# Where the output norm of the first linear-attention mixer is made: tile by tile inside its loop, or behind it

## The chip, the cores and the metric

The kernel runs on one core of one Trainium2 chip, in one launch. The metric is the device time of a run in microseconds (us); of the kernel before there are three runs, and their median counts. Beside them stands one profiled execution, from which all durations below are taken. PE is TensorE, PEld its weight loads, DVE VectorE, ACT ScalarE, POOL GpSimd and SP SyncE, which here issues most of the DMAs.

## The reference

The model has two layers on 512 tokens of width 1024. Layer 0 mixes the tokens with two linear attentions side by side, layer 1 with a sliding-window attention, and a mixture of 16 experts stands behind either. The change is in the first of the two linear attentions (gla below), whose chunks hold 64 tokens, with 4 heads of 64 key and 128 value columns:

```python
def gla_chunked(q, k, v, g):
    b = jnp.cumsum(g, axis=-2)
    b_last = b[..., -1:, :]
    q_dec = q * jnp.exp(b)
    k_dec = k * jnp.exp(-b)
    a = jnp.where(incl, jnp.einsum('bhnid,bhnjd->bhnij', q_dec, k_dec), 0.0)
    o_intra = jnp.einsum('bhnij,bhnjv->bhniv', a, v)
    upd = jnp.einsum('bhncd,bhncv->bhndv', k * jnp.exp(b_last - b), v)
    ...                        # state = dec * state + upd, chunk by chunk
    return o_intra + jnp.einsum('bhncd,bhndv->bhncv', q_dec, s_prev)

    ...
    oa = rms_norm(oa, gla_norm) * jax.nn.silu(za...)     # per token and head, over 128 values
    ...
    return o @ w_out
```

`rms_norm(x, gain)` is `x * rsqrt(mean(x*x) + 1e-6) * gain`. The norm of `oa` and its product with the gate are what the change moves.

## The kernel before

The kernel goes through stages one behind another. Between two stages PE, ACT and DVE each drain and wait for one another (the semaphore `phase_done`). The gla stage is the second of them, between the projection of layer 0 and the second linear attention (gdn). The order of the instructions on each engine is that in which the code is written, one program for each engine, with semaphores between them; `Steps` objects count them, and `X.at(t, name)` is the value at which step `name` of tile t is done.

The gla stage works on four tiles t of 128 tokens, each of two chunks c of 64. PSUM has eight banks of 128x512 words. In the loop over t:

- PE turns queries and keys of the next tile into bank 6 (`gla_turn`, L934, waits for `kz` of the tile before), multiplies the masked scores with the values into bank t (L1093, waits for `A`), adds the part of the state for chunk 0 (L1103, `int0`), makes the scores of the next tile in bank 7 (`gla_scores`, L1069), adds the part of the state for chunk 1 (L1103, `int1`, waits for `s0`), and makes the state's updates of the next tile in banks 4 and 5 (`gla_updates`, L1078). The second of these waits for `s1` of this tile, since DVE still reads bank 5 until then.
- DVE masks the scores (`A`, L2233), scales the next tile's queries and keys (`gla_qk`, L2212 and L2216), brings the state over chunk 0 (`s0`, L2241, four instructions, waits for `int0`), makes the next tile's scaled key rows (`gla_k_rows`, L2223, two instructions), and brings the state over chunk 1 (`s1`, L2241, waits for `int1`).
- ACT squares the four heads of bank t with their sums (`gla_sq`, `sm_g[:, 0]`, waits for `int1`). It does nothing else in the loop. All ACT instructions stand on L1566, a helper.

Behind the loop DVE first does one step of another job, the sums of a modulation vector (`mix_sides(1)`, L2055; its inputs come by SP, the load for the step three further on waits for this one). Then comes the norm of all four tiles at once: DVE `var` (L2250, 128x16), ACT the inverse root, DVE a Newton step of four instructions (`newton`, L2032, L2034, L2036, L2038, each waiting for the one before), then DVE 16 products of output, root and gate into `on_g` (L2257, 128x128 each, out of bank t), PE four transposes for each tile into bank 4+t (L934, waiting for `on` of the tile), and ACT a copy of each into `oT` (128x512). `on_g` holds the gate `silu(za)` times the gain beforehand. In the names of the profile `on_g` is in ring, `sm_g` and the state in work, `oT` in hT.

Of the kernel before, what the change touches and what calls it, by code (L numbers as in the profile page):

```python
# [15 lines left out]
P = 128  # L16
# [4 lines left out]
EPS = 1e-6  # L21
# [94 lines left out]
def build_block(nc, a, out):  # L116
    ctx = ExitStack()
    with ctx:
# [147 lines left out]
        GLA_PE = Steps(sem("gla_pe"), ["o", "int0", "int1"])  # L266
        GLA_DVE = Steps(sem("gla_dve"), ["A", "s0", "s1"])
        GLN_PE = Steps(sem("gla_norm_pe"), ["oT"])
        GLN_ACT = Steps(sem("gla_norm_act"), ["ss0", "ss1", "ss2", "ss3", "root", "oT0", "oT1", "oT2", "oT3"])
        GLN_DVE = Steps(sem("gla_norm_dve"), ["var", "n1", "n2", "n3", "rstd", "on0", "on1", "on2", "on3"])  # L270
        PRE_DVE = Steps(sem("gdn_pre_dve"), ["u", "au", "mx", "g", "lnb", "lk", "lq", "lbk", "pre", "colj"])
        PRE_ACT = Steps(sem("gdn_pre_act"), ["e", "l", "expa", "lnss", "exp"])
        PRE_PE = Steps(sem("gdn_pre_pe"), ["cum"])
# [656 lines left out]
        def _(pe):  # L930
# [141 lines left out]
            def gla_updates(t):  # L1072
                pe.wait_ge(GLP_DVE.sem, GLP_DVE.at(t, "ku"))
                for c in range(2):
# [4 lines left out]
                                 start=True, stop=True)  # L1079
                    ins.then_inc(GLP_PE.sem, GLP_PE.one(f"u{c}"))  # L1080

            def gla():

                gla_gates()
# [3 lines left out]
                for t in range(TT):  # L1088
# [16 lines left out]
                        ins.then_inc(GLA_PE.sem, GLA_PE.one(f"int{c}"))  # L1105
                    if t + 1 < TT:
                        gla_updates(t + 1)
                for t in range(TT):
                    pe.wait_ge(GLN_DVE.sem, GLN_DVE.at(0, f"on{t}"))
                    for hd in range(HEADS):  # L1110
                        ins = turn(bank(4 + t)[:, cols(hd)], on_g[:, t, hd])
                    ins.then_inc(GLN_PE.sem, GLN_PE.one("oT"))

            def gdn_pre():
                pe.wait_ge(PRE_DVE.sem, PRE_DVE.at(0, "g"))
# [448 lines left out]
        def _(act):  # L1564
# [140 lines left out]
            def gla():  # L1705
                act.wait_ge(const_in, 16)
                act.wait_ge(GATE_PE.sem, GATE_PE.at(0, "z"))
                f(gate_a, ps[:, 2:4].rearrange("p a b -> p (a b)"), ACT.Abs).then_inc(GATE_ACT.sem, GATE_ACT.one("abs"))
                act.wait_ge(GATE_ACT.sem, GATE_ACT.at(0, "abs"))
                f(gate_e, gate_a, ACT.Exp, scale=-1.0).then_inc(GATE_ACT.sem, GATE_ACT.one("e"))  # L1710
                act.wait_ge(GATE_ACT.sem, GATE_ACT.at(0, "e"))
                f(gate_e, gate_e, ACT.Ln, bias=1.0).then_inc(GATE_ACT.sem, GATE_ACT.one("l"))
                act.wait_ge(GATE_PE.sem, GATE_PE.at(0, "cums"))
                f(eb_all, ps[:, 4:8, 0:256], ACT.Exp, scale=1.0 / 16).then_inc(GATE_ACT.sem, GATE_ACT.one("eb"))
                f(enb_all, ps[:, 4:8, 0:256], ACT.Exp, scale=-1.0 / 16).then_inc(GATE_ACT.sem, GATE_ACT.one("enb"))
                f(ekb_all, ps[:, 4:8, 256:512], ACT.Exp, scale=1.0 / 16).then_inc(GATE_ACT.sem, GATE_ACT.one("ekb"))
                table(ACT.Abs_reciprocal_sqrt)
                for t in range(TT):
                    act.wait_ge(GLA_PE.sem, GLA_PE.at(t, "int1"))
                    for hd in range(HEADS):  # L1720
                        ins = f(gla_sq[:, t, cols(hd)], bank(t)[:, cols(hd)], ACT.Square,
                                accum_out=sm_g[:, 0, HEADS * t + hd:HEADS * t + hd + 1])
                    ins.then_inc(GLN_ACT.sem, GLN_ACT.one(f"ss{t}"))
                act.wait_ge(GLN_DVE.sem, GLN_DVE.at(0, "var"))
                f(sm_g[:, 2], sm_g[:, 1], ACT.Abs_reciprocal_sqrt).then_inc(GLN_ACT.sem, GLN_ACT.one("root"))
                for t in range(TT):
                    act.wait_ge(GLN_PE.sem, GLN_PE.at(t, "oT"))
                    f(oT[:, 0:HEADS, cols(t)], bank(4 + t, HEADS, P)).then_inc(GLN_ACT.sem, GLN_ACT.one(f"oT{t}"))

            def gdn_pre():  # L1730
                act.wait_ge(PRE_DVE.sem, PRE_DVE.at(0, "au"))
# [295 lines left out]
        def _(dve):  # L2027
# [191 lines left out]
            def gla_k_rows(t):  # L2219
# [3 lines left out]
                    ins = v.tensor_tensor(ku[r, t % 2, c], pqk[r, t, 256:512], ekb_all[r, t], ALU.mult)  # L2223
                ins.then_inc(GLP_DVE.sem, GLP_DVE.one("ku"))

            def gla():
                gla_gates()
                gla_qk(0)
# [2 lines left out]
                for t in range(TT):  # L2231
                    dve.wait_ge(GLP_PE.sem, GLP_PE.at(t, "A"))
                    v.copy_predicated(at_g, mask, bank(7, HEADS, P)).then_inc(GLA_DVE.sem, GLA_DVE.one("A"))  # L2233
                    if t + 1 < TT:
                        gla_qk(t + 1)
                    for c in range(2):
# [7 lines left out]
                        ins.then_inc(GLA_DVE.sem, GLA_DVE.one(f"s{c}"))  # L2244
                        if c == 0 and t + 1 < TT:
                            gla_k_rows(t + 1)
                        dve.wait_ge(GLA_DVE.sem, GLA_DVE.at(t, f"s{c}"))
                mix_sides(1)
                dve.wait_ge(GLN_ACT.sem, GLN_ACT.at(0, "ss3"))
                v.tensor_scalar(sm_g[:, 1], sm_g[:, 0], 1.0 / DV, EPS, ALU.mult, ALU.add).then_inc(GLN_DVE.sem, GLN_DVE.one("var"))  # L2250
                dve.wait_ge(GLN_ACT.sem, GLN_ACT.at(0, "root"))
                dve.wait_ge(GLN_DVE.sem, GLN_DVE.at(0, "var"))
                newton(GLN_DVE, 0, sm_g[:, 2], sm_g[:, 1], sm_g[:, 3])
                for t in range(TT):
                    for hd in range(HEADS):
                        n = HEADS * t + hd
                        ins = v.scalar_tensor_tensor(out=on_g[:, t, hd], in0=bank(t)[:, cols(hd)], scalar=sm_g[:, 2, n:n + 1],  # L2257
                                                     in1=on_g[:, t, hd], op0=ALU.mult, op1=ALU.mult)
                    ins.then_inc(GLN_DVE.sem, GLN_DVE.one(f"on{t}"))

            def gdn_pre():
                D_ = PRE_DVE
# [652 lines left out]
```

## Time and profile before

| | us |
|---|---|
| runs of the kernel, median of 3 | 1502.57 |
| lowest and highest of them | 1500.47, 1505.88 |
| the profiled execution, its own time | 1498.98 |
| its span in the trace | 1496.8 |
| the loop over t and the norm behind it, to the last copy | about 298 to 334 |

The span is the time from the first to the last instruction in the trace; 2.2 us of the profiled execution lie around it. A row of the timeline is a run of like instructions: its start, the time from the first's start to the last's end, engine, line, operation, the tiles out<-in, the count, and in brackets the idle time of the engine before it with what ended that.

### The profile page before, as it was taken

How to read it: one execution, taken by the hardware profiler on the slowest of the kernel's cores; microseconds unless marked ns; L12 is line 12 of the kernel's file. 1: busy time of each engine (PE TensorE's matmuls, PEld its weight loads, DVE VectorE, ACT ScalarE, POOL GpSimd, SP SyncE). 2: the span in 40 equal slices, each digit the busy share in tenths (PEclk: the TensorE clock that was granted, in tenths of full speed). 3: DMA queues.
4: the chain of work that ended last, by engine and by line, in shares of the span. 5: the costliest groups of instructions: out<-in, count | busy, mean ns of one | idle time of the engine just before them, and what ended most of it. 6: DMA issues, size and time to landing. Idle time of an engine off the chain costs nothing. (4 is left out here: it accounts for less than half of the span.)

```text
span 1496.8 us, 15648 instructions
## 1 busy us (share of the span) xinstructions
PE 1297.0 (87%) x6072; PEld 988.4 (66%) x6072; DVE 1090.4 (73%) x1325; ACT 699.3 (47%) x894; POOL 335.6 (22%) x130
## 2 busy tenths in 40 slices
PE   4799889566989986999999977986898699999992
PEld 1488777346986455888888864443445588888882
DVE  3757766575876464898899966777346499999994
ACT  2212332324135132777777743225613277777770
POOL 2100000000000001466666520000000145445541
PEclk9779999797999977999999997997997799999996
DMA  9678433701030254899999927346006489999954
GB/s 339 236 258 288 157 99 120 259 23 63 15 127 31 111 217 178 326 392 386 382 382 378 350 80 299 113 159 233 1 28 236 143 333 380 376 377 391 383 201 183
DMA packets 63888, 338.17 MB, mean 226 GB/s; under 512 B 11866, under 2 KB 12394, under 8 KB 49732
## 3 DMA queue, kind: packets, MB, share of 16 engines
q1 hardware_dynamic: 51428, 311.00, 55.7%
q0 software_dynamic: 11568, 22.91, 4.4%
q10 hardware_dynamic: 816, 3.23, 0.6%
q8 instruction: 50, 0.82, 0.2%
q14 instruction: 26, 0.21, 0.0%
HBM read 325.63 MB, written 28.84 MB: 237 GB/s over the span
## 5 line engine op out<-in xcount | busy, mean ns | idle before, releaser
L1410 PE MATMUL ps<-ring_r,work_r 128*128 128x512 f32 x536 | 211.5, 395 | 0.0
L830 POOL TENSOR_TENSOR work<-work,early_mod 128x1024 f32<-128x1024 f32 x30 | 169.7, 5656 | 145.5 <-ACT work L1566 145.5
L2434 DVE TENSOR_TENSOR ring_r<-ring,early_mod_r 128x2048 fp32r<-128x2048 f32 x76 | 182.4, 2433 | 27.1 <-ACT early_mod_r L1566 26.6
L1408 PE MATMUL ps<-early_mod_r,work_r 128*128 128x512 f32 x468 | 187.9, 401 | 7.7 <-DVE work_r L2737 4.7
L1409 PE MATMUL ps<-early_mod_r,work_r 128*128 128x512 f32 x468 | 183.6, 392 | 0.0
L1566 ACT ACTIVATE work<-ps 128x512 f32<-128x512 f32 (+4 forms) x123 | 80.2, 663 | 214.2 <-PE ps L1410 133.4
L1566 ACT ACTIVATE work_r<-ring 128x2048 fp32r<-128x2048 f32 (+2 forms) x87 | 133.5, 1557 | 55.4 <-PE ps L943 55.4
L934 PE MATMUL ps<-const,work 128*128 128x128 f32 x712 | 106.4, 292 | 49.6 <-DVE work L2550 12.2
L1566 ACT ACTIVATE early_mod_r<-ring 128x2048 fp32r<-128x2048 f32 x79 | 147.6, 1911 | 0.3 <-PE ps L1410 0.2
L934 PEld LDWEIGHTS ps<-const,work 128*128 128x128 f32 x712 | 90.1, 150 | 74.1 <-issue 14.7
L1408 PE MATMUL ps<-work_r 128*128 128x512 f32 x324 | 131.5, 406 | 6.8 <-DVE work_r L2737 4.7
L2434 DVE TENSOR_TENSOR ring_r<-ring,work_r 128x2048 fp32r<-128x2048 f32 x52 | 124.1, 2413 | 5.6 <-ACT work_r L1566 5.6
L1409 PE MATMUL ps<-work_r 128*128 128x512 f32 x324 | 128.1, 395 | 0.0
L1410 PEld LDWEIGHTS ps<-ring_r,work_r 128*128 128x128 f32 x536 | 102.0, 190 | 22.5
L1278 PE MATMUL ps<-ring,hT 128*128 128x512 f32 x256 | 111.1, 593 | 1.4 <-ACTq L2018 0.7
L1408 PEld LDWEIGHTS ps<-early_mod_r,work_r 128*128 128x128 f32 x468 | 88.3, 189 | 28.4 <-DVE work_r L2737 7.1
L822 POOL DMA_INDIRECT work<-h_rows,row_i x32 | 66.8, 2087 | 165.6 <-PE ps L934 118.1
L1409 PEld LDWEIGHTS ps<-early_mod_r,work_r 128*128 128x128 f32 x468 | 88.6, 189 | 17.1
L1278 PEld LDWEIGHTS ps<-ring,hT 128*128 128x128 f32 x256 | 48.2, 190 | 60.9 <-issue 58.4
L1302 PE MATMUL ps<-ring,hT 128*128 128x512 f32 x192 | 86.1, 608 | 1.9 <-ACT hT L1566 1.9
L1566 ACT ACTIVATE work_r<-ps 128x512 fp32r<-128x512 f32 (+1 forms) x66 | 53.5, 812 | 66.2 <-PE ps L934 66.2
L835 POOL DMA_DIRECT2D h_rows<-work x8 | 4.3, 541 | 348.2 <-DVE work L2424 348.2
(331 smaller groups left out, 2575.4 us busy)
## 6 DMA issues: line engine op xcount, KB each, us to landing
ring<-in_moe_w_up_dram SPq DMA_DIRECT2D x33, 2048.0 KB, 9.9
early_mod<-in_ada_w_dram SPq DMA_DIRECT2D x80, 512.0 KB, 4.6
ring<-in_moe_w_gate_dram SPq DMA_DIRECT2D x19, 2048.0 KB, 9.3
hT<-in_moe_w_down_dram SPq DMA_DIRECT2D x16, 2048.0 KB, 9.0
ring<-in_moe_w_down_dram SPq DMA_DIRECT2D x15, 2048.0 KB, 9.6
work<-in_moe_w_gate_dram SPq DMA_DIRECT2D x14, 2048.0 KB, 10.1
ring<-in_ab_w_in_dram SPq DMA_DIRECT2D x7, 2048.0 KB, 9.5
ring<-in_ada_w_dram SPq DMA_DIRECT2D x4, 2048.0 KB, 23.3
```

What stands on the lines that cost most here:

```text
L822: nc.gpsimd.indirect_dma_start(xg[buf], None, h_rows[l], bass.IndirectOffsetOnAxis(rows_, 0), bounds_check=SEQ - 1, oob_is_err=False).then ...
L830: return nc.gpsimd.tensor_tensor(yb[buf], yb[buf], mod[:, 5 * D:6 * D], ALU.mult)
L835: nc.gpsimd.dma_start(h_rows[l][P * t:P * t + P, :], h[:, t]).then_inc(h_out, 16)
L934: return nc.tensor.transpose(dst, src, ident[0:k, 0:k])
L1278: ins = mm(bank((2 * t + n) % 3), oT[:, k, cols(t)], slot(c0 + n)[:, k], start=(k == 0), stop=(k == 7))
L1302: ins = mm(bank(j % 4), hT[:, k, cols(t)], slot(c)[:, k], start=(k == 0), stop=(k == 7))
L1408: mm(out, a_lo, w_hi, start=first_, stop=False)
L1409: mm(out, a_hi, w_hi, start=False, stop=False)
L1410: return mm(out, a_hi, w_lo, start=False, stop=last_)
L1566: return nc.scalar.activation(out, in_, fn, **kw)
L2434: v.tensor_tensor(half_of(l, m, half, True), half_of(l, m, half), highs[(2 * m + half) % MHIGHS].bitcast(F32), ALU.subtract).then_inc(SV.s ...
```

## The change

The norm is made for each tile by itself, one tile behind the loop, in place of all four behind it.

- DVE: `output_variance(t - 1)` stands behind the mask of tile t, `output_norm(t - 1)` (the Newton step on 128x4, and four of the 16 products) behind the key rows and ahead of `s1` of tile t. Behind the loop and behind `mix_sides(1)` stand both for the last tile.
- ACT: behind the squares of tile t it waits for `var` of that tile, makes its root, and copies the transposed output of tile t-1. Behind the loop it copies that of the last tile.
- PE: the four transposes of tile t-1 stand behind the updates of tile t+1, and go into bank t-1 in place of bank 4+t-1. Those of the last tile stand behind the loop.

The root and the Newton step are now made four times on four columns and not once on 16: DVE has 12 more instructions of the Newton step and 3 more of the variance, ACT 3 more roots.

```diff
-        GLN_ACT = Steps(sem("gla_norm_act"), ["ss0", "ss1", "ss2", "ss3", "root", "oT0", "oT1", "oT2", "oT3"])
-        GLN_DVE = Steps(sem("gla_norm_dve"), ["var", "n1", "n2", "n3", "rstd", "on0", "on1", "on2", "on3"])
+        GLN_ACT = Steps(sem("gla_norm_act"), ["ss", "root"])
+        GLN_DVE = Steps(sem("gla_norm_dve"), ["var", "n1", "n2", "n3", "rstd", "on"])
...
+            def turn_output_a(t):
+                pe.wait_ge(GLN_DVE.sem, GLN_DVE.at(t, "on"))
+                for hd in range(HEADS):
+                    ins = turn(bank(t)[:, cols(hd)], on_g[:, t, hd])
+                ins.then_inc(GLN_PE.sem, GLN_PE.one("oT"))
...
                     if t + 1 < TT:
                         gla_updates(t + 1)
-                for t in range(TT):
-                    pe.wait_ge(GLN_DVE.sem, GLN_DVE.at(0, f"on{t}"))
-                    for hd in range(HEADS):
-                        ins = turn(bank(4 + t)[:, cols(hd)], on_g[:, t, hd])
-                    ins.then_inc(GLN_PE.sem, GLN_PE.one("oT"))
+                    if t:
+                        turn_output_a(t - 1)
+                turn_output_a(TT - 1)
...
+                def put_output(t):
+                    act.wait_ge(GLN_PE.sem, GLN_PE.at(t, "oT"))
+                    f(oT[:, 0:HEADS, cols(t)], bank(t, HEADS, P))
+
                 for t in range(TT):
                     act.wait_ge(GLA_PE.sem, GLA_PE.at(t, "int1"))
                     for hd in range(HEADS):
                         ins = f(gla_sq[:, t, cols(hd)], bank(t)[:, cols(hd)], ACT.Square,
                                 accum_out=sm_g[:, 0, HEADS * t + hd:HEADS * t + hd + 1])
-                    ins.then_inc(GLN_ACT.sem, GLN_ACT.one(f"ss{t}"))
-                act.wait_ge(GLN_DVE.sem, GLN_DVE.at(0, "var"))
-                f(sm_g[:, 2], sm_g[:, 1], ACT.Abs_reciprocal_sqrt).then_inc(GLN_ACT.sem, GLN_ACT.one("root"))
-                for t in range(TT):
-                    act.wait_ge(GLN_PE.sem, GLN_PE.at(t, "oT"))
-                    f(oT[:, 0:HEADS, cols(t)], bank(4 + t, HEADS, P)).then_inc(GLN_ACT.sem, GLN_ACT.one(f"oT{t}"))
+                    ins.then_inc(GLN_ACT.sem, GLN_ACT.one("ss"))
+                    act.wait_ge(GLN_DVE.sem, GLN_DVE.at(t, "var"))
+                    own = slice(HEADS * t, HEADS * t + HEADS)
+                    f(sm_g[:, 2, own], sm_g[:, 1, own], ACT.Abs_reciprocal_sqrt).then_inc(GLN_ACT.sem, GLN_ACT.one("root"))
+                    if t:
+                        put_output(t - 1)
+                put_output(TT - 1)
...
                     v.copy_predicated(at_g, mask, bank(7, HEADS, P)).then_inc(GLA_DVE.sem, GLA_DVE.one("A"))
+                    if t:
+                        output_variance(t - 1)
                     if t + 1 < TT:
                         gla_qk(t + 1)
...
                         if c == 0 and t + 1 < TT:
                             gla_k_rows(t + 1)
+                        if c == 0 and t:
+                            output_norm(t - 1)
                         dve.wait_ge(GLA_DVE.sem, GLA_DVE.at(t, f"s{c}"))
                 mix_sides(1)
...
+                output_variance(TT - 1)
+                output_norm(TT - 1)
```

The order of DVE's instructions in the middle turn t = 1, before: mask, next tile's queries and keys, `s0`, key rows, `s1`, and the mask of t = 2.

```order
L2233 COPY_PREDICATED work<-early_mod,ps 128x512 [waits gla_prep_pe,gla_dve]
L2212 SCALAR_TENSOR_TENSOR work<-ps,ring 128x256 [waits gla_prep_pe]
L2216 TENSOR_TENSOR early_mod<-ps,ring 64x256 x2
L2241 SCALAR_TENSOR_TENSOR work<-work,ring,ps 64x128 [waits gla_pe]
L2241 SCALAR_TENSOR_TENSOR work<-work,ring,ps 64x128 x3
L2223 TENSOR_TENSOR work<-work,ring 64x256 x2
L2241 SCALAR_TENSOR_TENSOR work<-work,ring,ps 64x128 [waits gla_pe,gla_dve]
L2241 SCALAR_TENSOR_TENSOR work<-work,ring,ps 64x128 x3
```

And in the changed kernel, from the mask of t = 1 to the first instruction of `s1` (L2258 is the mask, L2238 the variance, L2268 `s0` and `s1`, L2232 the key rows, L2041 to L2047 the Newton step, L2247 the products).

```order
L2258 COPY_PREDICATED work<-early_mod,ps 128x512 [waits gla_prep_pe,gla_dve]
L2238 TENSOR_SCALAR work<-work 128x4 [waits gla_norm_act]
L2221 SCALAR_TENSOR_TENSOR work<-ps,ring 128x256 [waits gla_prep_pe]
L2225 TENSOR_TENSOR early_mod<-ps,ring 64x256 x2
L2268 SCALAR_TENSOR_TENSOR work<-work,ring,ps 64x128 [waits gla_pe]
L2268 SCALAR_TENSOR_TENSOR work<-work,ring,ps 64x128 x3
L2232 TENSOR_TENSOR work<-work,ring 64x256 x2
L2041 TENSOR_TENSOR work<-work 128x4 [waits gla_norm_dve,gla_norm_act]
L2043 TENSOR_TENSOR work<-work 128x4 [waits gla_norm_dve]
L2045 TENSOR_SCALAR work<-work 128x4 [waits gla_norm_dve]
L2047 TENSOR_TENSOR work<-work 128x4 [waits gla_norm_dve]
L2247 SCALAR_TENSOR_TENSOR ring<-ps,work,ring 128x128 [waits gla_norm_dve]
```

Four Newton instructions and four products (the last three of them follow in a row of their own) have come between the key rows and `s1`.

PE's instructions at the end of the turn t = 1, before: the updates of tile 2 for chunk 1, the turn of tile 3's queries and keys, and the scores times values of tile 2.

```order
L1078 MATMUL ps<-work 128x256 [waits gla_dve]
L1078 MATMUL ps<-work 128x256
L934 MATMUL ps<-const,work 128x128 [waits gla_prep_dve]
L934 MATMUL ps<-const,work 128x128 x3
L1093 MATMUL ps<-work 128x128 [waits gla_dve]
```

And in the changed kernel (L1099 stands where L1093 did).

```order
L1078 MATMUL ps<-work 128x256 [waits gla_dve]
L1078 MATMUL ps<-work 128x256
L934 MATMUL ps<-const,ring 128x128 [waits gla_norm_dve]
L934 MATMUL ps<-const,ring 128x128 x3
L934 MATMUL ps<-const,work 128x128 [waits gla_prep_dve]
L934 MATMUL ps<-const,work 128x128 x3
L1099 MATMUL ps<-work 128x128 [waits gla_dve]
```

The four transposes of tile 0's output have come between the updates and the next tile's turn; the same four for tile 1 stand in the next turn ahead of the scores times values of tile 3, and those of tile 2 behind the last `int1`.

## Rows read from the trace of the kernel before

**Rows 1.** The page: the span, and one DMA group with its median us to landing
```profile
span 1496.8 us, 15648 instructions
...
early_mod<-in_ada_w_dram SPq DMA_DIRECT2D x80, 512.0 KB, 4.6
```
**Rows 2.** The timeline, all engines, the turn t = 1 of the loop
```profile
303.38 1.13 PE L1078 MATMUL ps<-work 128*128 128x256 f32 x4 [0.53 <-DVE work L2241]
...
304.34 0.60 PE L934 MATMUL ps<-const,work 128*128 128x128 f32 x4
...
304.78 1.06 PE L1093 MATMUL ps<-work 128*128 128x128 f32 x8
...
305.77 1.08 PE L1103 MATMUL ps<-work 128*64 128x256 f32 x4
...
306.77 1.16 PE L1069 MATMUL ps<-work,early_mod 128*128 128x128 f32 x8
306.88 1.43 DVE L2241 SCALAR_TENSOR_TENSOR work<-work,ring,ps 64x128 f32<-64x128 f32 x4 [0.71 <-PE ps L1103]
308.34 0.85 DVE L2223 TENSOR_TENSOR work<-work,ring 64x256 f32<-64x256 f32 x2
...
308.37 1.08 PE L1103 MATMUL ps<-work 128*64 128x256 f32 x4 [0.43 <-DVE work L2241]
...
309.55 1.43 DVE L2241 SCALAR_TENSOR_TENSOR work<-work,ring,ps 64x128 f32<-64x128 f32 x4 [0.36 <-PE ps L1103]
...
311.03 1.13 PE L1078 MATMUL ps<-work 128*128 128x256 f32 x4 [0.53 <-DVE work L2241]
```
**Rows 3.** The timeline again, the last turn and the norm behind the loop
```profile
321.76 1.43 DVE L2241 SCALAR_TENSOR_TENSOR work<-work,ring,ps 64x128 f32<-64x128 f32 x4 [2.35 <-PE ps L1103]
...
323.24 1.08 PE L1103 MATMUL ps<-work 128*64 128x256 f32 x4 [1.52 <-DVE work L2241]
...
324.43 1.43 DVE L2241 SCALAR_TENSOR_TENSOR work<-work,ring,ps 64x128 f32<-64x128 f32 x4 [1.24 <-PE ps L1103]
...
327.54 0.18 DVE L2032 TENSOR_TENSOR work<-work 128x16 f32<-128x16 f32 x1 [0.28 <-ACT work L1566]
...
328.38 4.23 DVE L2257 SCALAR_TENSOR_TENSOR ring<-ps,work,ring 128x128 f32<-128x128 f32 x16
329.56 3.98 PE L934 MATMUL ps<-const,ring 128*128 128x128 f32 x16 [5.25 <-DVE ring L2257]
...
330.71 0.60 ACT L1566 ACTIVATE hT<-ps 128x512 f32<-128x512 f32 x1 [3.20 <-PE ps L934]
...
333.58 0.60 ACT L1566 ACTIVATE hT<-ps 128x512 f32<-128x512 f32 x1 [0.21 <-PE ps L934]
```
**Rows 4.** Groups by line and form: busy us, mean ns of one
```profile
L2257 DVE SCALAR_TENSOR_TENSOR ring<-ps,work,ring 128x128 f32<-128x128 f32 x16 | 4.2, 345 | 0.0
...
L2038 DVE TENSOR_TENSOR work<-work 128x4 f32<-128x4 f32 x4 | 0.6, 162 | 0.1
```
**Rows 5.** The timeline: DMA issues on SP, and small instructions of the next stage
```profile
327.20 10.28 SPq L712 DMA_DIRECT2D early_mod<-in_ada_w_dram  x2
...
335.85 4.06 DVE L2055 SCALAR_TENSOR_TENSOR x<-early_mod,par,x 128x1024 f32<-128x1024 f32 x3
...
343.21 0.17 DVE L2286 TENSOR_TENSOR work<-ps,work 128x16 f32<-128x16 f32 x1
343.30 0.17 DVE L2287 TENSOR_TENSOR work<-ps,work 128x16 f32<-128x16 f32 x1
```
**Rows 6.** Stretches: us, busy us of PE, PEld, DVE, ACT, POOL, PEclk, DMA, GB/s
```profile
322.00:324.00 2.00, 0.76 (x4) 0.47 (x4) 1.14 (x4) 0.00 (x0) 0.00 (x0) 1.00 0.00 0
...
328.00:330.00 2.00, 0.44 (x2) 0.44 (x3) 1.93 (x9) 0.00 (x0) 0.00 (x0) 0.50 0.72 207
...
350.00:355.00 5.00, 5.00 (x46) 5.00 (x45) 1.31 (x5) 1.02 (x2) 0.00 (x0) 0.98 0.00 0
```
**Rows 7.** The timeline: the scores of tile 0, ahead of the loop, at the lower clock
```profile
292.43 2.07 PE L1069 MATMUL ps<-work,early_mod 128*128 128x128 f32 x8 [1.28 <-DVE early_mod L2216]
```

More of the change, by code:

```diff
@@ L2224, in gla_k_rows, with output_variance, output_norm @@
                 ins.then_inc(GLP_DVE.sem, GLP_DVE.one("ku"))
+            def output_variance(t):
+                own = slice(HEADS * t, HEADS * t + HEADS)
+                dve.wait_ge(GLN_ACT.sem, GLN_ACT.at(t, "ss"))
+                v.tensor_scalar(sm_g[:, 1, own], sm_g[:, 0, own], 1.0 / DV, EPS, ALU.mult, ALU.add).then_inc(GLN_DVE.sem, GLN_DVE.one("var"))
+            def output_norm(t):
+                own = slice(HEADS * t, HEADS * t + HEADS)
+                dve.wait_ge(GLN_ACT.sem, GLN_ACT.at(t, "root"))
+                dve.wait_ge(GLN_DVE.sem, GLN_DVE.at(t, "var"))
+                newton(GLN_DVE, t, sm_g[:, 2, own], sm_g[:, 1, own], sm_g[:, 3, own])
+                for hd in range(HEADS):
+                    n = HEADS * t + hd
+                    ins = v.scalar_tensor_tensor(out=on_g[:, t, hd], in0=bank(t)[:, cols(hd)], scalar=sm_g[:, 2, n:n + 1],
+                                                 in1=on_g[:, t, hd], op0=ALU.mult, op1=ALU.mult)
+                ins.then_inc(GLN_DVE.sem, GLN_DVE.one("on"))
             def gla():
@@ L2246, in gla @@
                             gla_k_rows(t + 1)
+                        if c == 0 and t:
+                            output_norm(t - 1)
                         dve.wait_ge(GLA_DVE.sem, GLA_DVE.at(t, f"s{c}"))
                 mix_sides(1)
[L2249 to L2259, printed above, removed]
+                output_variance(TT - 1)
+                output_norm(TT - 1)
             def gdn_pre():
```

## The prediction

> **What bounds the kernel now.** The page's shares of busy time are means over a span of 1496.8 us [rows 1] and say little on a stage of some 36 us, so the reading goes to the timeline of the stage itself. In a middle turn of the loop [rows 2] one takes the second updates' start (303.38) and follows who starts next: turn of queries and keys 304.34, scores times values 304.78, `int0` 305.77, then DVE's `s0` 306.88, PE's `int1` 308.37, DVE's `s1` 309.55, and the second updates of the next tile 311.03. The turn lasts 7.65 us (0.96 + 0.44 + 0.99 + 1.11 + 1.49 + 1.18 + 1.48), and each link waits for the one before: the brackets of `s0`, `int1`, `s1` and the updates all name the partner engine. It is a ring of PE and DVE, in which neither is the sole bound. So what the loop has to give is not DVE's or PE's idle time in sum, but the idle time at the very place where something is put in. Between the key rows and `s1` DVE is idle for 0.36 us; on PE between the updates, the turn and the scores times values there is none.
>
> Behind the loop [rows 3] DVE is the bound: `s1` of the last tile at 324.43, the step of the other job, the Newton step from 327.54, the 16 products from 328.38 to 332.61. PE's transposes follow the products tile by tile, and ACT's four copies follow those, the last from 333.58 to 334.18. PE, ACT and DVE must all be through before the next stage, so the last copy ends the stage. No transfer is waited for in this stretch, and the stages behind it begin with waits of the engines for one another, so a shift of this end should go through to the end of the kernel nearly whole.
>
> **The change, in the loop on DVE.** `var` of the tile before falls into the wait for the turn of queries and keys, and is hidden. ACT's root follows it by more than 2 us before it is needed, and is hidden too. The Newton step and the four products are not: they stand between the key rows and `s1`. Four Newton instructions took 328.38 - 327.54 = 0.84 us with their waits for one another [rows 3], on 128x16; those on 128x4 last 162 ns each [rows 4], about 0.01 us less, so I take 0.80. The 16 products took 4.23 us, the last one's own 345 ns included, so one starts (4.23 - 0.345) / 15 = 0.259 us behind the other [rows 3, 4], four of them 1.04. Together 1.84 us are put in. Key rows end at 309.19; `s1` would start at 311.03 in place of 309.55: **1.48 us later**, in the turns t = 1 and t = 2 [rows 2]. In the last turn there are no key rows: `s0` ends at 323.19, plus 1.84 is 325.03 in place of 324.43: **0.60 us later** [rows 3]. Nothing takes the delay of `s1` in: behind it wait the second updates, and behind those on PE's queue all of the next tile. On DVE the next mask is behind it; it starts right behind `s1` as the updates do, and PE has updates and a turn (1.40 us) to do before it asks for it.
>
> **In the loop on PE.** Four transposes of a tile take 0.44 us from the start of one group to the next [rows 2]. They stand in the ring at t = 1 and t = 2, between the updates and the next tile's work: 2 x 0.44 = **0.88 us**. PE never waits for `on` there, since the products are ahead of `s1`, for which the updates have waited. Those of tile 2, behind the last `int1`, wait for `on` at about 325.0, and nothing is behind them but the last tile's: no cost. ACT's copy of tile t-1 (0.60 us) falls into waits of several us for `int1`: none either.
>
> The loop becomes longer by 2 x 1.48 + 0.60 + 0.88 = **4.44 us**.
>
> **Behind the loop.** From `s1` of the last tile on, the same chain runs, but with 4 products in place of 16. The last tile's transposes stand where tile 0's stood, 329.56, and the copy where tile 0's stood, 330.71 to 331.31. In place of 334.18 that is **2.87 us less** [rows 3]; DVE's saving of 12 products is 12 x 0.259 = 3.11, and 0.24 of it goes since the first copy came 1.15 us behind its transposes' start and the last one less. The Newton step is shorter by 0.04.
>
> **The queues.** No DMA is moved. SP's load behind the step of the other job was issued at 327.20, when that step's DVE instruction had freed its buffer, and is used by the third of the three steps at 335.85 and later, about 338.4 [rows 5]. Both are shifted alike by the loop, but the use comes 2.9 us nearer; a gap of 11 us becomes one of 8, which hides a load of 4.6 us to landing [rows 1]. If that cover were gone, the next stage would wait on it.
>
> **The sum.** 4.44 - 2.87 - 0.04 = +1.5 us. Of the profiled execution's 1498.98 us (2.2 us of it outside the span) that makes 1500.5. That execution lies 3.6 us below the median of the runs; carried over to this, 1502.57 + 1.5 = **1504.1 us**.
>
> Bounds. Below: the Newton instructions at their bare 0.16 us each, 0.64, and the tail saving the full 3.11: 2 x 1.32 + 0.44 + 0.88 - 3.1 = +0.9. Above: the products at 0.345 each, which is how the four of `s1` follow one another (1.43 for four), and the transposes of a tile at 1.0 us as in the tail, where the clock was 0.50 and DVE paced them: 0.84 + 1.38 = 2.22 put in, 2 x 1.86 + 0.98 + 2 x 1.0 - 2.4 = +4.3. I take the middle turn's rows since it is the place and the clock. To either side comes the clock of the next stage. There PE works without a gap, at 0.50 until about 350 and at 0.98 behind it [rows 6]; where the rise falls against the work is not set by the program alone, and a shift of 3 us in it would be worth 1.5 us.
>
> **What a page says against the small instructions' price.** A Newton instruction here costs 0.20 to 0.21 us from start to start though it has 4 or 16 columns [rows 3, 4]. The Trainium skill, page "VectorE: DVE Perf Modes", section "The TRN2 errata — SBUF-src ops pay a fixed extra latency per instruction", gives 58 cycles plus the columns for an instruction from SBUF to SBUF at 0.96 GHz, thus by estimate 0.065 us for four columns, and 120 plus the columns out of PSUM, 0.26 us for a product. For the product the trace agrees (0.259); for the small ones it shows three times as much, and by the page's figure the sum would come out near -0.6: it would speak for the first rival below. The trace's figure is taken.
>
> **Rivals.**
>
> *The small instructions run closer.* Those that don't depend on one another start 0.09 us apart [rows 5]. If the four cost no more than that, the Newton step would put in 0.36 in place of 0.80: 2 x 1.04 + 0.16 + 0.88 = 3.1, less 2.87 and less 0.48 in the tail: **-0.2 us, 1502.4**. Against it: each of them reads what the one before wrote and waits for its semaphore, and in the tail they did stand 0.21 apart. 7%.
>
> *The clock falls in the longer waits.* PE's wait for `s1` grows from 0.53 to about 2.0 us in the turns 1 and 2, and its waits in a turn from 0.96 of 7.65 us to 2.44 of 9.57 [rows 2]. Should the chip answer with the lower clock, the scores would take 2.07 us where they take 1.16 [rows 7, 2], a factor of 1.8. PE's own links in the ring (0.96, 0.44, 0.44, 0.99, about 1.0 and 1.0) are 4.8 us in a turn; at the lower clock for the rest of the loop, two turns, that costs 2 x 4.8 x 0.8 = 7.7 on top: +9, **1511.8**. For a single fall of some 4 us it is +3 on top: +4.5, **1507.1**. This is the case that ends slower than before, and it decides from the point at which more than about half a turn runs low. Against it: in the last turn before the change PE waits 1.52 us and is busy for 0.76 of 2 us, and the granted clock is still 1.00 there; it fell only later, in the 5.25 us without work [rows 3, 6]. The Trainium skill, page "TensorE: Matmul & The Clock Gate", section "A second HAM failure mode: psum-queue depth-cycling", tells of a kernel in which short idle times between groups of matmuls alone were enough to make the clock swing; by that rule this case would be the likely one, and no row here shows such a swing. 9%.
>
> *The gain is the larger part.* For the time to fall by more than 0.3% the norm would have to be hidden altogether: even then only the tail's 2.9 us are won, under the 4.5 that a measurement can tell. So a faster result can come only from elsewhere (clock or spread of the runs): 3%.
>
> **How the numbers follow.** The forecast (+0.9 to +4.3) has 80%, the closer small instructions 7%, the clock 9%, and 4% are left for shifts elsewhere. The bound of what can be told from no change is 0.3%, 4.5 us: above 1507.1 or below 1498.1. Slower: the clock's 9% and 3% of the forecast's upper end with a spread of runs against it: 12%. Faster 3%. Same 85%. The range goes from the lower bound, less 1.5 for the next stage's clock and 1.5 for the runs' spread (1500.5 to 1505.9 before), 1500.2, to the upper bound, plus as much of these as two independent terms make together: 1502.6 + 4.3 + 2.0 = 1508.9, which takes in the single fall of the clock.
>
> **What the changed profile would show.** Right: `s1` at t = 1 starts 4.15 us behind `s0` (2.67 before), and `s0` of the next tile comes 9.6 us behind it (in place of 7.65); the four transposes stand 0.44 us between updates and turn; PEclk 1.0 in the loop; behind the last `s1` the last copy ends 6.9 us later, not 9.75. Wrong: `s1` no later than before, so that the Newton step and products were free; PEclk under 0.9 between `s0` of t = 1 and the last `int1`; a table load on ACT between squares, roots and copies (none stands in the changed order, but each would be on the way to the root); or a wait for a load in the next stage.

## The result, and the profile after

The changed kernel takes 1505.9 us (median of 20 runs, 1501.74 to 1509.87), the one before 1502.46 (20 runs, 1498.02 to 1507.06). The ratio is 1.0024, with a 95% interval of 1.0014 to 1.0034: 3.6 us longer, 2.1 to 5.1. It is slower, by less than the 0.3% that was set as the bound; of the forecast of +1.5 us the sign is right, but the size is less than half of what was measured, and +1.5 lies outside the interval. The profiled execution took 1507.7 us. Its page:

```profile
span 1505.6 us, 15669 instructions
```

The timeline of the turn t = 1, all engines, from `s0` of this tile to `s0` of the next (L2268 `s0` and `s1`, L2232 key rows, L2041 the first Newton instruction, L2247 products, L1078 updates, L934 transposes, L1099 scores times values, L1109 `int0`). It answers to [rows 2]:

```profile
307.67 1.43 DVE L2268 SCALAR_TENSOR_TENSOR work<-work,ring,ps 64x128 f32<-64x128 f32 x4 [0.71 <-PE ps L1109]
...
309.13 0.85 DVE L2232 TENSOR_TENSOR work<-work,ring 64x256 f32<-64x256 f32 x2
...
310.01 0.16 DVE L2041 TENSOR_TENSOR work<-work 128x4 f32<-128x4 f32 x1
...
310.81 1.13 DVE L2247 SCALAR_TENSOR_TENSOR ring<-ps,work,ring 128x128 f32<-128x128 f32 x4
...
311.85 1.42 DVE L2268 SCALAR_TENSOR_TENSOR work<-work,ring,ps 64x128 f32<-64x128 f32 x4
...
313.33 1.65 PE L1078 MATMUL ps<-work 128*128 128x256 f32 x4 [2.04 <-DVE work L2268]
...
314.76 1.06 PE L934 MATMUL ps<-const,ring 128*128 128x128 f32 x4
...
315.62 1.06 PE L934 MATMUL ps<-const,work 128*128 128x128 f32 x4
...
316.47 1.41 PE L1099 MATMUL ps<-work 128*128 128x128 f32 x8
...
317.81 1.08 PE L1109 MATMUL ps<-work 128*64 128x256 f32 x4
...
318.93 1.43 DVE L2268 SCALAR_TENSOR_TENSOR work<-work,ring,ps 64x128 f32<-64x128 f32 x4 [1.03 <-PE ps L1109]
```

Between `s0` and `s1` lie 4.18 us in place of 2.67; the bracket of the updates, 2.04, was 0.53. Then come PE's four links, and they are slow: updates to transposes 1.43 us where [rows 2] has 0.96, transposes 0.86 and turn 0.85 where it has 0.44, scores times values 1.34 where it has 0.99. One turn later the same groups run at the old pace:

```profile
324.58 1.13 PE L1078 MATMUL ps<-work 128*128 128x256 f32 x4 [2.03 <-DVE work L2268]
...
325.55 0.60 PE L934 MATMUL ps<-const,ring 128*128 128x128 f32 x4
...
325.99 1.06 PE L1099 MATMUL ps<-work 128*128 128x128 f32 x8
```

The stretches of the changed kernel say why (columns as in [rows 6]; PEclk is the third from the end). PE is idle, the clock still full; then it is at half while PE works without a gap; then full again to the last `int1`:

```profile
312.00:313.00 1.00, 0.00 (x0) 0.00 (x0) 0.96 (x4) 0.00 (x0) 0.00 (x0) 1.00 0.00 0
314.00:317.00 3.00, 3.00 (x14) 2.71 (x13) 0.37 (x3) 0.80 (x2) 0.00 (x0) 0.50 0.00 0
318.00:332.00 14.00, 9.13 (x48) 5.85 (x47) 9.77 (x34) 3.09 (x18) 0.00 (x0) 1.00 0.00 0
```

Behind the loop, the rows that answer to [rows 3]: the last `s1`, the first Newton instruction, the products, the transposes, the copy, and the first instruction of the next stage.

```profile
331.39 1.42 DVE L2268 SCALAR_TENSOR_TENSOR work<-work,ring,ps 64x128 f32<-64x128 f32 x4
...
334.48 0.16 DVE L2041 TENSOR_TENSOR work<-work 128x4 f32<-128x4 f32 x1 [0.27 <-ACT work L1570]
...
335.27 1.13 DVE L2247 SCALAR_TENSOR_TENSOR ring<-ps,work,ring 128x128 f32<-128x128 f32 x4
...
336.45 1.11 PE L934 MATMUL ps<-const,ring 128*128 128x128 f32 x4 [4.27 <-DVE ring L2247]
...
337.60 0.60 ACT L1570 ACTIVATE hT<-ps 128x512 f32<-128x512 f32 x1 [2.67 <-PE ps L934]
...
338.39 0.48 DVE L2866 MEMSET work<- 128x512 f32 x1 [2.00 <-ACTq L1994]
```

From the last `s1` to that memset are 7.00 us; in the kernel before they are 334.39 - 324.43 = 9.96.

A measure of the stage that leaves out what differs ahead of it is the time from `s0` of tile 0 to the memset. The two rows of before, and the first of the changed kernel:

```profile
299.23 1.43 DVE L2241 SCALAR_TENSOR_TENSOR work<-work,ring,ps 64x128 f32<-64x128 f32 x4 [0.71 <-PE ps L1103]
...
334.39 0.48 DVE L2846 MEMSET work<- 128x512 f32 x1 [1.78 <-ACTq L1985]
```
```profile
300.02 1.43 DVE L2268 SCALAR_TENSOR_TENSOR work<-work,ring,ps 64x128 f32<-64x128 f32 x4 [0.71 <-PE ps L1109]
```

That is 38.37 us against 35.16, **+3.21**. It divides into: `s1` later by 1.51 in two turns and by 0.63 in the last (3.30 us behind `s0`, before 2.67), the tail 2.96 less, and the rest, from `s1` to the next `s0`: 7.08 and 4.98 us against 4.99 and 4.56.

### The profile page after: what moved, and what is told of

Same layout as the page of the kernel before. It is cut to its first block and busy times, and to the rows that moved or that the text cites. A ratio compares the mean times of both kernels' runs of the same rounds, so it can differ in the third digit from the quotient of the medians.

```text
span 1505.6 us, 15669 instructions
## 1 busy us (share of the span) xinstructions
PE 1299.5 (86%) x6072; PEld 991.5 (66%) x6072; DVE 1100.1 (73%) x1340; ACT 699.2 (46%) x897; POOL 314.6 (21%) x130
## 5 line engine op out<-in xcount | busy, mean ns | idle before, releaser
L2454 DVE TENSOR_TENSOR ring_r<-ring,early_mod_r 128x2048 fp32r<-128x2048 f32 x76 | 191.2, 2546 | 26.9 <-ACT early_mod_r L1570 26.4
L830 POOL TENSOR_TENSOR work<-work,early_mod 128x1024 f32<-128x1024 f32 x30 | 149.1, 4968 | 143.5 <-ACT work L1570 143.5
L934 PE MATMUL ps<-const,work 128*128 128x128 f32 x712 | 108.5, 296 | 49.5 <-DVE work L2570 12.2
L934 PEld LDWEIGHTS ps<-const,work 128*128 128x128 f32 x712 | 91.6, 153 | 73.4 <-issue 13.9
L826 POOL DMA_INDIRECT y_rows<-work,dest_i x32 | 72.6, 2269 | 34.4 <-POOL work L830 23.2
```

Source lines behind the costliest of these rows:

```text
L826: nc.gpsimd.indirect_dma_start(y_rows[l], bass.IndirectOffsetOnAxis(rows_, 0), yb[buf], None, bounds_check=2 * SEQ - 1, oob_is_err=False). ...
L830: return nc.gpsimd.tensor_tensor(yb[buf], yb[buf], mod[:, 5 * D:6 * D], ALU.mult)
L934: return nc.tensor.transpose(dst, src, ident[0:k, 0:k])
L2454: v.tensor_tensor(half_of(l, m, half, True), half_of(l, m, half), highs[(2 * m + half) % MHIGHS].bitcast(F32), ALU.subtract).then_inc(SV.s ...
```

## The experiments

Two theories stood against each other for the part that the forecast lacked. A: PE's waits of 2 us for `s1` bring the clock down, and with it PE's links of the ring. B: the clock falls in this stage by chance, whatever the waits are (for the delay alone B is another one, named there). Stage is the measure above, tail the time from the last `s1` to the memset; ratios are to the kernel before on the same chip, with the 95% interval. Where a row has several values, they are of several traces, in the order in which they were taken.

| kernel | stage us | tail us | falls of the clock in the loop | ratio of times |
|---|---|---|---|---|
| before (three traces) | 35.16, 35.36, 35.16 | 9.96, 10.15, 9.96 | none | 1 |
| changed (three traces) | 38.37, 38.42, 38.38 | 7.00, 7.01, 7.01 | one in each, turn 1 | 1.0024 (1.0014 to 1.0034), 1.0013 (1.0000 to 1.0025) |
| transposes behind the loop | 38.64 | 6.55 | two | 1.0010 (0.9988 to 1.0032) |
| filled wait | 36.72 | 7.01 | none | 1.0001 (0.9990 to 1.0012) |
| delay alone | 41.03 | 10.19 | two | 1.0033 (1.0018 to 1.0048) |
| norm early | 33.43, 33.43 | 7.02, 7.01 | none | 1.0003 (0.9990 to 1.0016), 0.9992 (0.9981 to 1.0003) |
| norm spread | 32.45, 32.46 | 7.02, 7.02 | none | 0.9981 (0.9966 to 0.9996), 0.9968 (0.9953 to 0.9982) |

**The two kernels again.** Of the kernel before:

> The kernel before, looked at once more. The stage is measured from the start of s0 of tile 0 to the first memset of the next stage: 35.2 us in the first look (299.23 to 334.39). Theory A (the waits of the changed loop let the clock fall): again 35.2 within 0.3, PEclk 1.00 from s0 of tile 0 to the last int1. Theory B (the clock falls by chance, whatever the waits): in some look of this kernel too a stretch of 0.50 stands in the loop, and the stage is then 1 to 2 us longer.

> The kernel before, a third look. Theory A: stage 35.2 to 35.4, PEclk 1.00 to the last int1.

Of the changed kernel:

> The changed kernel again. Its stage was 38.4 us (300.02 to 338.39): by the sum 35.2 + 2 x 1.51 + 0.63 + 2 x 0.44 - 2.96 = 36.8, and 1.65 us more for a stretch of PEclk 0.50 at 313.9 to 317.1. Theory A: 36.8 with the clock at 1.00 throughout or 38.4 with one fall, which then lies behind a wait of 2 us for s1. Theory B: the same two values, the fall anywhere. By time 2 to 5 us above the kernel before.

> The changed kernel, a third look at the clock in its loop. Theory A: again a fall behind one of the two waits of 2 us for s1, stage 38.4 (or about 40 with a fall behind both, 36.8 with none).

In the three traces of the kernel before the clock stays full over the loop (here the third, all of it), in the three of the changed one it falls in the same turn each time (here the third as well):

```profile
298.00:324.00 26.00, 20.96 (x110) 14.15 (x108) 17.27 (x45) 4.03 (x29) 0.00 (x0) 1.00 0.00 0
```
```profile
312.00:313.00 1.00, 0.00 (x0) 0.00 (x0) 0.96 (x4) 0.00 (x0) 0.00 (x0) 1.00 0.00 0
314.00:316.00 2.00, 2.00 (x9) 1.71 (x8) 0.15 (x2) 0.31 (x2) 0.00 (x0) 0.50 0.00 0
```

Three of three against none of three speaks against chance, and for a fall that belongs to the first long wait; the kernels below carry this further. That it never followed the second one was not expected.

**The wait filled.** PE gets something to do in it, nothing else is changed:

```diff
                 for c in range(2):
+                    if c and t > 1:
+                        for n in range(14):
+                            turn(bank(3)[:, cols(n % 4)], ident)
                     if t:
                         pe.wait_ge(GLA_DVE.sem, GLA_DVE.at(t - 1, f"s{c}"))
```

> The changed kernel with 14 more transposes of the identity on PE between the first and the second updates of tiles 2 and 3 (into a bank not yet used), in the wait for s1; they take about 1.54 of its 2.04 us and put off nothing. Theory A: PEclk 1.00 through the whole loop, stage 36.8. Theory B: the clock falls as often as in the changed kernel, 38.4 where it does.

Of this kernel the timeline of PE in turn 1 (L1081 are the updates, L1102 scores times values, L1112 `int0`), and the stretch:

```profile
313.36 1.69 PE L934 MATMUL ps<-const 128*128 128x128 f32 x14
...
315.55 1.13 PE L1081 MATMUL ps<-work 128*128 128x256 f32 x4 [0.50 <-DVE work L2271]
...
316.52 0.60 PE L934 MATMUL ps<-const,ring 128*128 128x128 f32 x4
...
316.95 0.60 PE L934 MATMUL ps<-const,work 128*128 128x128 f32 x4
...
317.39 1.06 PE L1102 MATMUL ps<-work 128*128 128x128 f32 x8
```
```profile
312.00:322.00 10.00, 9.06 (x58) 6.74 (x56) 7.62 (x25) 1.95 (x10) 0.00 (x0) 1.00 0.00 0
```

The stage is 36.72 us, 36.8 were foretold by A. From `s1` to the next `s0` are 5.43 and 4.98 us: 0.44 and 0.42 more than in the kernel before, which is the price of the four transposes, and **1.65 us** less than the 7.08 of the changed kernel, which is the price of the fall. `s1` comes as late as in the changed kernel (4.17 us behind `s0`). So work that has no use took 1.65 us off the stage. Whether the time of the kernel followed is not shown: the ratio was 1.0001 where the changed kernel on the same chip had 1.0013, but the two intervals overlap by about half.

**The transposes and copies behind the loop, DVE's part left in it.**

```diff
-                    if t:
-                        turn_output_a(t - 1)
-                turn_output_a(TT - 1)
+                for t in range(TT):
+                    turn_output_a(t)
...
-                    if t:
-                        put_output(t - 1)
-                put_output(TT - 1)
+                for t in range(TT):
+                    put_output(t)
```

> The transposes and ACT's copies of all tiles stand behind the loop again, the norm on DVE stays in the loop. If the transposes cost 0.44 us each time in the ring, the stage is 35.9 us without a fall of the clock (36.8 - 0.88), about 37.2 with one. If they were hidden anyway: 36.8 without. Those of tiles 0 to 2 run under the last s1 and the step of the other job, so the tail is that of the changed kernel (7.0 us from the last s1 to the memset).

A miss: 38.64 us, longer than the changed kernel though less stands in the ring. The clock fell behind both waits; the stretches (the first line is in the first wait and the second behind it, the third is in the second wait and the fourth behind it):

```profile
314.00:316.00 2.00, 0.11 (x1) 0.12 (x2) 1.92 (x7) 0.00 (x0) 0.00 (x0) 1.00 0.00 0
...
317.00:319.00 2.00, 2.00 (x10) 1.89 (x9) 0.79 (x3) 0.00 (x0) 0.00 (x0) 0.50 0.00 0
325.00:326.00 1.00, 0.00 (x0) 0.00 (x0) 0.97 (x5) 0.00 (x0) 0.00 (x0) 1.00 0.00 0
327.00:329.00 2.00, 2.00 (x7) 1.65 (x7) 0.41 (x2) 0.20 (x1) 0.00 (x0) 0.50 0.00 0
```

From `s1` to `s0` are 6.59 and 6.17 us, 1.60 and 1.61 above the kernel before; without the two falls the stage would be 35.4, 1.3 below the filled kernel: 0.86 for the transposes and 0.46 for the tail. The expectation had one fall and the changed kernel's tail; here the clock was still full at the last transposes, and they took 0.66 us in place of 1.11. Whether the second wait brings a fall is thus not settled by its length: with the transposes in the ring it did not in three traces, without them it did in one.

**The delay alone.** In the kernel before, seven products that nothing uses stand where the norm stands in the changed one, for the tiles 1 and 2; the norm stays behind the loop. (The semaphore only orders the products among themselves.)

```diff
                             gla_k_rows(t + 1)
+                        if c == 0 and t in (1, 2):
+                            for n in range(7):
+                                if n == 4 or (n == 0 and t == 2):
+                                    dve.wait_ge(delay_done, 2 * t - 2 + n // 4)
+                                ins = v.scalar_tensor_tensor(out=gla_sq[:, 3, cols(n % 4)], in0=bank(3)[:, cols(n % 4)], scalar=1.0,
+                                                             in1=on_g[:, t - 1, n % 4], op0=ALU.mult, op1=ALU.mult)
+                                if n in (3, 6):
+                                    ins.then_inc(delay_done, 1)
```

> The kernel before, norm behind the loop as it was, with seven products (128x128, out of an idle bank, into a scratch) between key rows and s1 of the tiles 1 and 2 that nothing uses: they put off s1 by 1.5 us each, as the norm does in the changed kernel, and leave everything else. Theory A: the wait alone brings the fall: stage 35.3 + 2 x 1.5 = 38.3, plus 1 to 1.7 us for a stretch of PEclk 0.50 behind one of the two waits, thus 39.3 to 40. Theory B (the fall has to do with the transposes, the bank or ACT's part of the change): 38.3 with PEclk 1.00.

Here the timeline of PE behind the first of the two waits, and the stretches in the first wait, behind it, and behind the second:

```profile
311.46 1.56 PE L1079 MATMUL ps<-work 128*128 128x256 f32 x4 [1.72 <-DVE work L2242]
312.81 1.06 PE L935 MATMUL ps<-const,work 128*128 128x128 f32 x4
313.66 1.91 PE L1094 MATMUL ps<-work 128*128 128x128 f32 x8
```
```profile
310.00:312.00 2.00, 0.54 (x3) 0.49 (x4) 1.92 (x6) 0.00 (x0) 0.00 (x0) 1.00 0.00 0
313.00:315.00 2.00, 2.00 (x12) 2.00 (x11) 1.08 (x3) 0.00 (x0) 0.00 (x0) 0.50 0.00 0
...
323.00:325.00 2.00, 2.00 (x9) 1.82 (x9) 0.00 (x0) 0.00 (x0) 0.00 (x0) 0.50 0.00 0
```

The seven put off `s1` by 1.20 us each (3.87 behind `s0`), not by 1.5, and the stage missed the 39.3 to 40 of A on the long side: both waits, of 1.72 and 1.71 us, brought a fall, where one had been foretold, worth 1.65 and 1.59 us between `s1` and the next `s0`. 35.16 + 2 x 1.20 + 3.24 + 0.23 in the tail = 41.03, as measured. So the wait alone is enough: a fall needs neither the transposes nor the banks nor ACT's new order. B, which here put it down to these, falls. In the filled kernel DVE did the changed kernel's work in these waits and nothing fell, so it is PE's idle time that brings the fall, and not DVE's work in it.

**The norm early.** Its variance ahead of the mask, Newton step and products ahead of the next queries and keys, PE and ACT as in the changed kernel.

```diff
+                    if t:
+                        output_variance(t - 1)
                     dve.wait_ge(GLP_PE.sem, GLP_PE.at(t, "A"))
                     v.copy_predicated(at_g, mask, bank(7, HEADS, P)).then_inc(GLA_DVE.sem, GLA_DVE.one("A"))
                     if t:
-                        output_variance(t - 1)
+                        output_norm(t - 1)
...
-                        if c == 0 and t:
-                            output_norm(t - 1)
```

> The changed kernel with the norm of the tile before in another place on DVE: its variance ahead of the mask, Newton step and products behind the mask and ahead of the next queries and keys, where DVE waited 0.9 us for PE's turn and then 0.7 us for int0. Theory A (a place in the ring costs what it goes beyond the wait there, and the clock falls only behind waits of 2 us): from s1 to the next s0 DVE then has 0.15 + 0.73 + 1.84 + 1.19 = 3.9 us of work and PE, transposes included, 3.85; s0 comes about 0.4 us later than in the kernel before in the turns 1 and 2, s1 not at all later behind s0 (2.67 us), no fall of the clock; stage 35.3 + 0.8 - 3.0 = 33.1 us, thus about 2 us faster than the kernel before. Rival (the norm in the loop costs its own DVE time wherever it stands): stage 36.7.

> The version with the whole norm ahead of the queries and keys once more: its stage was 33.43 us, 1.8 less than in the kernel before, but its first comparison gave a ratio of 1.0003 (interval 0.9990 to 1.0016). If that was the spread of the runs, the two comparisons together lie about 0.9988; if the 1.8 us get lost behind the stage, it is again 1.000 or above, and some later stretch is longer by about 2 us in both traces.

The clock from ahead of `s0` of tile 0 to the start of the last `s1` (325.32), first trace:

```profile
298.00:326.00 28.00, 23.16 (x124) 15.67 (x122) 22.93 (x73) 5.99 (x35) 0.00 (x0) 1.00 0.00 0
```

The stage is 33.43 us both times, close to the 33.1 of A and far from the 36.7 of the rival. `s1` stands 2.67 us behind `s0` again; from `s1` to the next `s0` are 5.33, 5.43 and 4.99 us, 0.34, 0.44 and 0.43 more than before. The third of these had been taken for zero: PE's transposes are in the ring ahead of the last tile's scores times values too. In the time of the kernel the gain is not shown: the two comparisons together lie near 0.9997, and the 1.8 us of the stage should have made 0.9988. The next stage, from the memset to the load of x on SP, took 82.70 and 82.87 us where it took 82.31, 82.45 and 82.30 before, so some 0.4 us went there. The 1.4 us that are left would make 0.9991, which lies in both intervals, as 1.0 does.

**The norm spread over the waits.** On DVE `output_norm` is the Newton step alone, and the products of one tile stand in four places (`output_products(t, lo, hi)` makes those of the heads lo to hi - 1); on PE the transposes one turn later and ahead of `int1`, where PE waits for `s0`, on ACT the copies after them:

```diff
+                    if t > 1:
+                        output_products(t - 2, 3, 4)
+                    if t:
+                        output_variance(t - 1)
                     dve.wait_ge(GLP_PE.sem, GLP_PE.at(t, "A"))
                     v.copy_predicated(at_g, mask, bank(7, HEADS, P)).then_inc(GLA_DVE.sem, GLA_DVE.one("A"))
                     if t:
-                        output_variance(t - 1)
+                        output_norm(t - 1)
                     if t + 1 < TT:
                         gla_qk(t + 1)
+                    if t:
+                        output_products(t - 1, 0, HEADS if t + 1 == TT else 2)
...
-                        if c == 0 and t:
-                            output_norm(t - 1)
+                        if c == 0 and 0 < t < TT - 1:
+                            output_products(t - 1, 2, 3)
...
                                 gla_scores(t + 1)
+                            if t > 1:
+                                turn_output_a(t - 2)
+                            if t == TT - 1:
+                                turn_output_a(t - 1)
                             pe.wait_ge(GLA_DVE.sem, GLA_DVE.at(t, "s0"))
...
```

> The norm of the tile before cut into the waits of a turn: variance and the last product of the tile before that ahead of the mask, Newton step behind the mask, two products behind the next queries and keys, one behind the key rows, one behind s1; in the last turn all of it ahead of s0. PE's transposes stand one turn later, ahead of int1, where PE waits 0.43 us for s0; ACT's copies follow them. Theory A: no place goes beyond its wait by more than 0.1 us, so the turns stay at 7.65 us, the clock at 1.00, and the tail is the changed kernel's 7.0: stage 35.3 - 3.0 + 0.2 = 32.5 us, 2.8 us under the kernel before. Rival (own DVE and PE time counts wherever it stands): 36.7 or more.

> The spread version once more: its first comparison gave a ratio of 0.9981 (interval 0.9966 to 0.9996), its stage was 32.45 us against 35.2 and 35.4 in the kernel before. If the stage's 2.8 us reach the end of the kernel, the ratio is again between 0.997 and 0.9995, and the stage 32.5 with no fall of the clock.

Part of the turn t = 2 of this kernel (L2280 `s0` and `s1`, L2252 products, L934 transposes, L1113 `int1`):

```profile
314.31 0.61 DVE L2252 SCALAR_TENSOR_TENSOR ring<-ps,work,ring 128x128 f32<-128x128 f32 x2
...
314.89 1.43 DVE L2280 SCALAR_TENSOR_TENSOR work<-work,ring,ps 64x128 f32<-64x128 f32 x4
...
315.77 0.60 PE L934 MATMUL ps<-const,ring 128*128 128x128 f32 x4
...
316.37 1.08 PE L1113 MATMUL ps<-work 128*64 128x256 f32 x4
317.23 0.35 DVE L2252 SCALAR_TENSOR_TENSOR ring<-ps,work,ring 128x128 f32<-128x128 f32 x1
...
317.55 1.43 DVE L2280 SCALAR_TENSOR_TENSOR work<-work,ring,ps 64x128 f32<-64x128 f32 x4
```

`s1` is 2.66 us behind `s0`, the turns 0 and 1 last 7.66 us, where [rows 2] has 7.65, from `s0` of tile 2 to that of tile 3 are 7.44 us (7.22 before), `int1` (L1113) has no wait left in its row, and the transposes (L934 out of ring) lie in what was that wait. The stage is 32.45 and 32.46 us, 32.5 were foretold, 2.7 to 2.9 below the kernel before. The times follow: medians 1500.91 and 1497.04 us beside 1503.82 and 1501.43 of the kernel before in the same comparisons, both intervals below 1. This version is faster than the kernel before by 0.2% to 0.3%; its next stage, 81.77 and 81.79 us, gives another 0.5 to 0.7 us of that, for which no cause is shown. The changed kernel, above 1 in its two comparisons, was not run beside it.

## Why the prediction was right, and what it lacked

The median of 1505.9 us lies in the foretold range of 1500.2 to 1508.9, and the change stays within the 0.3% that were called the same. Most terms of the sum came as they were taken; one was missing.

- **`s1` later by 1.48 in two turns, 0.60 in the last**: 1.51 and 0.63. The Newton step took 310.81 - 310.01 = 0.80, the four products 1.04, as taken; 0.03 came from the gap behind the key rows. Right.
- **The transposes in the ring, 2 x 0.44**: 0.44 and 0.42 in the filled kernel. Right.
- **The tail 2.87 + 0.04 less**: 2.96. Right.
- **The price of a small instruction.** The four Newton instructions start 0.20 us apart in the loop as well, so the rival by which they run closer is out for this place. So is the figure of 58 cycles plus columns of the Trainium skill, "VectorE: DVE Perf Modes", section "The TRN2 errata — SBUF-src ops pay a fixed extra latency per instruction"; the same section says itself that this figure comes out too short for a single instruction.
- **The queues.** SP's load was used without a wait, no table load came up between squares, roots and copies. Right.
- **The clock: the term that failed.** The sum held nothing for it, and the rival had 9%. The evidence against it was that a wait of 1.52 us in the last turn had not lowered the clock, and it took a wait of 2.0 for like it. Waits of 1.72 and of 2.04 us did lower it. A single fall was priced at 3 us; it cost 1.65: four of PE's links grew from 2.83 to 4.48 us, and the rest of the turn ran at the full clock again. 1.5 + 1.65 = 3.2 is the stage's measured growth of 3.21. The Trainium skill, "TensorE: Matmul & The Clock Gate", section "A second HAM failure mode: psum-queue depth-cycling", speaks of short idle times between matmul groups that make the clock swing; this case's traces show that at waits of 1.7 to 2.0 us, and the prediction weighed the page too low.
- **A swing was there to be read.** The prediction says that no row shows one. Its own trace does, ahead of the loop: PE waits for 2.95 us, does four transposes, waits for 1.28 us more, and the clock, full until then, is at half for the scores of tile 0 [rows 7] and full again in the loop. All 13 traces of this case have a fall at that place, in one of these two waits.

```profile
290.49 0.66 PE L934 MATMUL ps<-const,work 128*128 128x128 f32 x4 [2.95 <-ACT ring L1566]
```
```profile
290.00:292.00 2.00, 0.66 (x4) 0.42 (x4) 0.80 (x3) 1.93 (x3) 0.00 (x0) 1.00 0.89 332
292.00:294.00 2.00, 1.57 (x7) 1.57 (x8) 1.21 (x3) 0.00 (x0) 0.00 (x0) 0.55 0.19 78
```

- **Its own signs.** `s1` 4.18 us behind `s0` (4.15 foretold) and the last copy's end 6.81 us behind the last `s1` (6.9) came. The next `s0` stood 11.26 us behind `s0` and not 9.6, the transposes took 0.86 and not 0.44 at t = 1, and a stretch at 0.50 stood between `s0` of t = 1 and the last `int1`, where the sign of being wrong was a clock under 0.9 (the mean over all of it is 0.92).
- **Luck in the number.** That +3.6 lies below the forecast's upper bound of +4.3 owes nothing to the terms this bound was made of, slower products and transposes paced by DVE, which did not come; the fall that came instead happened to cost half its price. The width of the range was not worked out cleanly either: below, 1502.57 + 0.9 - 3.0 is 1500.5 and not 1500.2, and the 2.4 us of the tail in the upper bound are not derived from any row.
- **The rest goes through, as far as can be told.** The stage's +3.2 are at 4.4 us when layer 0's experts are loaded, 482.18 before and 486.54 after, of which 0.8 came from ahead of the stage and 0.4 from behind it. The measured +3.6 (2.1 to 5.1) agrees, but is too wide to show that nothing is lost on the way.

The span of the profiled executions differs by 8.8 us, though, and that is another matter; the last section has it.

## What to carry to other kernels

Where two engines hand work to one another in a ring, a piece put into one of them costs what it exceeds the wait at that very place, and not its share of idle time: with DVE's part ahead of `s1` the norm and its transposes cost 1.5 + 0.4 us in a middle turn, with it ahead of the queries and keys 0.3 to 0.4, and cut to the waits' sizes nothing in the turn t = 1 and 0.2 in t = 2. Look then at what the other engine does meanwhile: a wait of TensorE that grows from 0.5 to 1.7 or 2 us can bring its clock down, and the work behind it pays again. Filling such a wait with transposes that nothing uses tells the two costs apart: here it left the wait's 1.5 us and took away the clock's 1.65.

## What the runs showed of the hardware

- In the loop, waits of PE of 1.7 us (two of two, the delay alone) and of 2.0 us (five of eight, the changed kernel and the one with its transposes behind the loop) were followed by a stretch at the lower of the two levels, 1.2 in place of 2.4 GHz, that began 0.1 to 0.7 us behind the moment at which PE took up work again; the wait of 1.52 us in the last turn never was. Each fall cost 1.6 to 1.7 us. What tells the waits of 2.0 us that brought none from the others stays open.
- The largest part of the difference between the two profiled executions is not shown to belong to the change. From the first expert load of layer 0 to the load of `sum_rows` behind it (SP, L761 and L781) the kernel before took 408.06, 408.23 and 413.34 us in three traces, the changed one 413.74, 408.04 and 413.81, always with the same program there; the other versions lie between 410.8 and 414.9. The rows of before and of after:

```profile
482.18 0.33 SPq L761 DMA_DIRECT2D ring<-in_moe_w_gate_dram  x1
...
890.24 0.34 SPq L781 DMA_DIRECT2D ring<-sum_rows  x1
```
```profile
486.54 0.33 SPq L761 DMA_DIRECT2D ring<-in_moe_w_gate_dram  x1
...
900.28 0.34 SPq L781 DMA_DIRECT2D ring<-sum_rows  x1
```

  5.7 of the 8.8 us between the two spans lie there. A comparison of single spans would have put them on the norm.
